# First attention of a transformer kernel: queries and keys split into high and low parts, scores in three passes

## What is computed

```python
h = rms_norm(x, norm_mix[l])
aq, ak, av, bq, bk, bv, cq = jnp.split(h @ w_in[l], offsets, axis=-1)
aq = rms_norm(aq.reshape(b, t, A_HEADS, 2, A_HEAD_DIM), a_q_norm[l])      # 4 heads, 2 components, 64
ak = rms_norm(ak.reshape(b, t, A_HEADS, 2, A_HEAD_DIM), a_k_norm[l])
...
def one_block(args):                                # 128 queries
    s = jnp.einsum('bqhcd,bkhcd->bhcqk', qb, k).astype(jnp.float32) * scale
    s = s - slopes[None, :, None, None, None] * dist[None, None, None]
    p = jax.nn.softmax(s, axis=-1)
    p_diff = p[:, :, 0] - lam * p[:, :, 1]
    return jnp.einsum('bhqk,bkhe->bqhe', p_diff.astype(v.dtype), v)
```

## Time and profile before

| | us |
|---|---|
| median of the 3 runs | 3133.65 |
| lowest and highest | 3133.06, 3135.37 |
| the profiled execution, its device time | 3138.5 |
| its span in the profile | 3136.7 |
| PE busy, of the span | 3070.3 |
| third attention with head 0's query and key tiles | from about 139 to 215 |
| first attention, first to last scores | 204 to 494 |

### The profile page before, as it was taken

One profiled execution on the slowest core, in us unless ns is written; L12 is line 12 of the kernel. 1 busy time (PEld: TensorE's weight loads), 2 busy tenths in 40 slices (PEclk: granted clock), 3 DMA queues, 4 the chain that ended last, 5 costly groups with the idle time before them and its releaser, 6 DMA issues.

```text
span 3136.7 us, 50320 instructions
## 1 busy us (share of the span) xinstructions
PE 3070.3 (98%) x18600; PEld 2611.5 (83%) x18600; DVE 1795.4 (57%) x3577; ACT 1333.8 (43%) x2641; POOL 648.6 (21%) x870
## 2 busy tenths in 40 slices
PE   7999999999999999999999999998999999999999
PEld 7988888999999888888788887887977777687777
DVE  6557674353344332345788886876353666753675
ACT  5446565454445221232333333455433555522452
POOL 3424334453541000001111111000101011032240
PEclk9999999999999999999999999999999999999999
DMA  5110011011111221122232225643100000221012
GB/s 204 37 48 18 21 36 51 28 62 51 59 49 54 95 77 51 51 106 79 73 111 106 101 101 200 201 150 132 53 28 22 16 28 15 108 68 70 28 61 101
DMA packets 77412, 231.27 MB, mean 74 GB/s; under 512 B 17712, under 2 KB 21936, under 8 KB 65648
## 3 DMA queue, kind: packets, MB, share of 16 engines
q1 hardware_dynamic: 77168, 228.05, 20.9%
HBM read 183.92 MB, written 43.84 MB: 73 GB/s over the span
## 4 chain that ended last, share of the span: by engine, by line
PE 89%; DVE 6%; ACT 2%; issue 1%; DMA 1%; SPq 0%; POOL 0%; DVEq 0%; ACTq 0%; POOLq 0%
PE ps L2545 70%; PE ps L2588 7%; PE ps L2596 3%; PE ps L2552 2%; PE ps L2603 2%; PE ps L2619 2%; PE ps L2611 1%; PE ps L2622 1%; PE ps L2639 1%; DVE wlo L2814 0%; DVE hlo L2891 0%; ACT hhi L2659 0%; DMA wd<-in_WD 0%; ACT whi L2649 0%; DVE qk L2922 0%
## 5 line engine op out<-in xcount | busy, mean ns | idle before, releaser
L2545 PE MATMUL ps<-whi,hhi 128*128 128x256 f32 (+2 forms) x1920 | 581.1, 303 | 1.4 <-DVE hlo L3016 1.0
L2545 PE MATMUL ps<-whi,hlo 128*128 128x256 f32 (+2 forms) x1920 | 564.4, 294 | 0.0
L2545 PE MATMUL ps<-wlo,hhi 128*128 128x256 f32 (+2 forms) x1920 | 564.2, 294 | 0.0
L2545 PEld LDWEIGHTS ps<-whi,hhi 128*128 128x128 f32 x1920 | 368.7, 192 | 11.2 <-issue 3.4
L2545 PEld LDWEIGHTS ps<-wlo,hhi 128*128 128x128 f32 x1920 | 369.1, 192 | 7.6 <-issue 0.2
L2545 PEld LDWEIGHTS ps<-whi,hlo 128*128 128x128 f32 x1920 | 368.6, 192 | 7.8
L3153 POOL TENSOR_SCALAR stats<-stats 128x2 f32<-128x2 f32 (+2 forms) x230 | 59.5, 259 | 1434.8 <-ACT xsf L2653 511.9
L2545 PE MATMUL ps<-hhi,whi 128*128 128x512 f32 x864 | 342.3, 396 | 0.0
L2545 PE MATMUL ps<-hhi,wlo 128*128 128x512 f32 x864 | 337.0, 390 | 0.0
L2545 PE MATMUL ps<-hlo,whi 128*128 128x512 f32 x864 | 336.3, 389 | 0.0
L3142 POOL CAST whi<-raw 128x512 fp32r<-128x512 f32 (+4 forms) x172 | 109.0, 634 | 649.8 <-PE ps L2545 640.4
(11 more groups left out here) (616 smaller groups left out, 7013.3 us busy)
## 6 DMA issues: line engine op xcount, KB each, us to landing
raw<-in_W SPq DMA_DIRECT2D x61, 1024.0 KB, 4.9
scratch_fs<-fo SPq DMA_DIRECT2D x77, 256.0 KB, 2.0
raw<-in_W SPq DMA_DIRECT2D x24, 768.0 KB, 4.2
wd<-in_WD SPq DMA_DIRECT2D x44, 256.0 KB, 3.3
wf0b<-in_WF SPq DMA_DIRECT2D x10, 1024.0 KB, 5.2
wf1b<-in_WF SPq DMA_DIRECT2D x10, 1024.0 KB, 5.2
scratch_x<-x SPq DMA_DIRECT2D x16, 512.0 KB, 3.4
orw<-scratch_outs SPq DMA_DIRECT2D x6, 1024.0 KB, 5.6
```

Source lines behind the costliest of these rows:

```text
L2545: x = e.matmul(r.out, a, b, start=(r.start and m == 0), stop=(r.stop and m == n - 1), skip_group_check=r.joined)
```

## The change

Queries and keys of the first attention are kept as a high and a low part of type fp32r, and a score group takes three passes (high keys by high queries, low by high, high by low) in the place of float32 products. Two blocks of 256 keys that lie side by side become one of 512: in 48 of the 64 groups; in 16 they stay two blocks. ACT writes the high part of each as before, and DVE makes the low part from PSUM and the high part, two new instructions of 128 columns for each of the 32 tiles; the second of these now sets free the turn's bank and tells that the tile is ready. The queries move from two whole heads to a ring of twelve tiles; the exponentials of the second component get buffers of their own (`aF`, two of 1024), `aE` is three of 1024, `aPT` two instead of three.

```diff
         def qk_out(q):
             q.frees = [flat(free() if callable(free) else free) for _, _, free in q.outs]
+            q.two = isinstance(q.outs[0][0], tuple)
+            q.hi_done = [signal("qk_hi") for _ in q.outs] if q.two else []
             emit("qk_out", q)
             q.done(q.turned.read)
...
                     u.ei, u.E, u.E_free = self.E.take()
+                    u.halves = [u.E]
+                    if self.E2.bufs:
+                        u.e2i, u.E2, free = self.E2.take()
+                        u.halves.append(u.E2)
+                        u.E_free = u.E_free + free
...
-        aq = [rest(f"aq{i}", [T], F, 8 * KB * i) for i in range(2)]
-        ak = [rest(f"ak{i}", [T], F, 8 * KB * i + 4 * KB) for i in range(2)]
+        aq = [[rest(f"aq{n}{i}", [128], R, o + 512 * n) for n in range(2)] for i, o in enumerate(aq_at)]
+        ak = [[rest(f"ak{i}{n}", [T], R, o[n] * KB) for n in range(2)] for i, o in enumerate(((0, 4), (36, 60)))]
...
-        aE = [rest(f"aE{i}", [2 * T], F, (40 + 8 * i) * KB) for i in range(3)]
-        aPT = [rest(f"aPT{i}", [T], F, (28 + 4 * i) * KB) for i in range(3)]
+        aE = [rest(f"aE{i}", [T], F, (40 + 4 * i) * KB) for i in range(3)]
+        aE2 = [rest(f"aF{i}", [T], F, (52 + 4 * i) * KB) for i in range(2)]
+        aPT = [rest(f"aPT{i}", [T], F, (28 + 4 * i) * KB) for i in range(2)]
...
-                qk_evac(t, p, 64, [(aq[h % 2][:, cut], aq_gain[:, h:h + 1], lambda: a_scored(h - 2)),
-                                   (ak[h % 2][:, cut], col("a_k_norm"), None)],
+                n = 8 * h + t
+                q_free = lambda: a_units[n - 12].s_full if n >= 12 else c_free
+                qk_evac(t, p, 64, [(tuple(x[:, :] for x in aq[n % 12]), aq_gain[:, h:h + 1], q_free),
+                                   (tuple(x[:, cut] for x in ak[h % 2]), col("a_k_norm"), lambda: a_scored(h - 2))],
...
-                        pieces.append(([q[half, cut]] * 2, [k[half, 256 * x:256 * x + 256] for x in res[p:p + 2]], bias))
+                        x, y = res[p:p + 2]
+                        keys = [sl(256 * x, 512)] if y == x + 1 else [sl(256 * x, 256), sl(256 * y, 256)]
+                        pieces.append(([tuple(w[half, :] for w in q)] * len(keys), [tuple(w[half, c_] for w in k) for c_ in keys], bias))
... (PE)
+                            for j, (a_, b_) in enumerate(((0, 0), (0, 1), (1, 0))):
+                                for p in r.parts:
+                                    q, k = p.blocks[b]
+                                    x = e.matmul(p.place.ps[:, o:o + n], q[a_], k[b_], start=j == 0, stop=j == 2)
... (ACT)
+                        if r.two:
+                            e.activation(dst[0], v, ACT.Copy, scale=gain).then_inc(w.sig(r.hi_done[x]), 1)
+                            continue
... (DVE)
+                elif kind == "qk_out" and r.two:
+                    for x, (dst, gain, _) in enumerate(r.outs):
+                        w.wait_ge(*w.last)
+                        w.wait_each(r.hi_done)
+                        v = r.turned.ps[:, x * 128:(x + 1) * 128]
+                        a = e.scalar_tensor_tensor(dst[1], v, gain, dst[0].bitcast(F), ALU.mult, ALU.subtract)
+                        a.then_inc(w.sig(r.turned.read) if x else w.inner(), 1)
```

More of the change, by code:

```diff
@@ L645, in build, with __init__ @@
         class Att:
-            def __init__(self, E, PT, os_, sb, ob, dve_turns=True, together=False, paired=False, by_feature=False, between=False):
+            def __init__(self, E, PT, os_, sb, ob, dve_turns=True, together=False, paired=False, by_feature=False, between=False, second=()):
                 self.by_feature, self.between = by_feature, between
@@ L657, in __init__ @@
                 self.dve_turns, self.together, self.paired = dve_turns, together, paired
-                self.turn = 0
+                self.turn, self.E2 = 0, Slots(second)
             def scores(self, *us):
@@ L683, in scored @@
                         r.blocks = list(zip(q, rhs)) if isinstance(q, list) else [(q, rhs)]
-                        r.n = sum(k.shape[-1] for _, k in r.blocks)
-                        r.out, r.mx = u.E[:, at_[x]:at_[x] + r.n], mxs[x][:, p:p + 1]
+                        r.n = sum(width(k) for _, k in r.blocks)
+                        r.out, r.mx = u.halves[comp.half][:, at_[x]:at_[x] + r.n], mxs[x][:, p:p + 1]
                         at_[x] += r.n
@@ L695, in scored @@
                     x_ = Rec()
-                    x_.u, x_.e, x_.scored, x_.mx = u, u.E[:, comp.col:at_[x]], r.place.read, mx
+                    x_.u, x_.e, x_.scored, x_.mx = u, u.halves[comp.half][:, comp.col:at_[x]], r.place.read, mx
                     if u.kept:
@@ L731, in combine @@
                 u.e_ready = [u.mixed]
+                self.E2.free[u.e2i] = [u.mixed]
             def probs(self, u):
@@ L823, in unit, with comp, width @@
             return u
-        def comp(col_, pieces):
+        def comp(col_, pieces, half=0):
             c = Rec()
-            c.col, c.pieces = col_, pieces
+            c.col, c.pieces, c.half = col_, pieces, half
             return c
+        def width(k):
+            return (k[0] if isinstance(k, tuple) else k).shape[-1]
         def post_plain(self, u):
@@ L1080, in build @@
             for qt in range(8):
-                q, k, tb = aq[h % 2], ak[h % 2], atab
+                q, k, tb = aq[(8 * h + qt) % 12], ak[h % 2], atab
                 res, at_ = key_order(qt)
-                cut = slice(qt * 128, (qt + 1) * 128)
                 comps = []
@@ L2585, in _ @@
                     for b in range(len(r.parts[0].blocks)):
-                        n = r.parts[0].blocks[b][1].shape[-1]
+                        n = width(r.parts[0].blocks[b][1])
+                        if isinstance(r.parts[0].blocks[b][0], tuple):
+                            for j, (a_, b_) in enumerate(((0, 0), (0, 1), (1, 0))):
+                                for p in r.parts:
+                                    q, k = p.blocks[b]
+                                    x = e.matmul(p.place.ps[:, o:o + n], q[a_], k[b_], start=j == 0, stop=j == 2)
+                                    if j == 2 and b == len(p.blocks) - 1:
+                                        x.then_inc(p.place.full[0], 1)
+                            o += n
+                            continue
                         for p in r.parts:
@@ L2934, in _ @@
                             if len(p.bias.shape) == 3:
-                                src, out = [a.rearrange("p (g c) -> p g c", g=len(p.blocks)) for a in (src, out)]
+                                src, out = [a.rearrange("p (g c) -> p g c", g=p.bias.shape[1]) for a in (src, out)]
                             x = e.tensor_tensor_reduce(out=out, in0=src, in1=p.bias, scale=-u.scale, scalar=3e38,
```

15 lines of the change are left out of this document (9 added, 6 removed).

## The result

| us | before | after |
|---|---|---|
| median, with the number of runs | 3135.26 (10) | 3143.72 (10) |
| lowest and highest | 3133.06, 3138.05 | 3141.77, 3146.54 |
| profiled execution: device time, span | 3138.5, 3136.7 | 3141.77, 3140.0 |
| first scores of the first attention | 204.46 | 211.92 |
| its last unit's second score group | 492.79 | 501.87 |

The changed kernel is slower: ratio of the times 1.0029, 95% interval 1.0021 to 1.0036, which is 8.5 us. The profiles put it where it was looked for: up to the first scores 7.46 us are lost, from there to the last unit's second group 1.62, together 9.08.

The account below looks back on a forecast made before the run. PE's queue was taken as the bound. Third attention +6.7, first attention's one-tile units +5.7, savings -5.6 and -0.3, head starts +1.0 gave +7.5 us on the median 3133.65: 3141 us; 8-in-10 range 3128 to 3153.

Parts of the forecast that it names:

- the bank's release at the turn of `cE`: Third attention, head 0: the bank has no slack, so PE stands still 0.84 us longer at 8 tiles, +6.7 us.
- the ring of ACT and DVE: First attention, units with one query-key tile: waits between ACT and DVE set 9.11 us against PE's 8.33; together +5.7 us.
- the step on two-tile units: First attention, six units with two query-key tiles: PE doesn't wait for DVE and each keeps the 0.35 us saving.
- Score groups: First attention: fp32r halves overlap, groups take 0.89 us, or 0.92 split, saving 0.35 us a unit.
- The low parts, each, and the third attention: DVE takes 0.351 us per low part; the bank is free 0.84 us after ACT's last high part, +6.7 us over 8 tiles.
- The ninth: First attention, one-tile unit behind the second head's start: starts with 0.8 us of slack, so costs 0.
- the waits spread: Rival, first attention: DVE's delay also reaches two-tile units and high parts wait longer; +5 on the sum, 3146 us, chance 0.07.
- Starts of heads: Second and fourth heads: scores wait for the last key tile; low parts add 0.84, the unit saves 0.35; +1.0 us together.
- halves halfway between together and in turn: Rival, score groups: an fp32r pair takes 0.34 us, about +17 for the groups, 3153 us; chance 0.07.
- only the third attention pays: Rival: first attention's ACT-DVE waits are looser, PE keeps all 11 us there; -4.5 us, 3129 us, chance 0.20.
- no wait shows: Rival: waits in the first and third attention stay hidden and only the passes count; 3122 us, chance 0.06.
- halves in turn: Rival, score groups: array halves alternate in fp32r, groups take 1.58 and 1.64 us; 3176 us, chance 0.10.

Follow-up runs that it names:

- low parts from a copy: Changed kernel, but ACT writes float32 copies to SBUF and frees the bank; high and low parts are made from the copy: 3139.56 us, ratio 1.0016 to before.
- the form with both moves: Copy-based kernel with the last two tiles of heads 1 to 3 made directly from PSUM, and ACT's copied high parts behind the square: 3131.99 us, ratio 0.9989 to before.
- The form with the one move alone: Copy-based kernel with the last two tiles of heads 1 to 3 made directly from PSUM, ACT's high parts still ahead of the square: 3134.06 us, ratio 0.9995 to before.

## Why the prediction was right

It said 3141, +7.5 us, slower; the time is +8.5 in the medians, +9.1 at the end of the stage in the traces. The measured 3143.72 lies 2.7 above the 3141, and 1.6 of these are the median of before, which rose from 3133.65 to 3135.26 with more runs. The two mechanisms on which it rests, the bank's release at the turn of `cE` and the ring of ACT and DVE, are what the runs show. That the sum came so near is in part luck: the step on two-tile units was wrong by 2.2 us, and the ring came out 1.3 us better than said. By its own steps:

- *Score groups.* 0.89 and 0.92 us were said, 0.89 and 0.91 measured. The row that was nearest, the same group in float32, told it; the share of the page didn't. The saving of 0.35 us a unit comes nearly in full where nothing waits: 0.31 to 0.34 in ten of the 12 units with other tiles, 0.17 and 0.18 in the two shortest. The sum had 11.2 for all units; without low parts the profiles show 9.1 in this stage, and the 12 us between the medians are more than that.
- *The low parts, each, and the third attention.* 0.351 us each, all 64 of them alike. 0.84 us for a tile became 0.87, and 6.7 became 6.87 (low parts in head 0 alone) to 7.46. Doubling them moved the first scores by 6.33, for 6.2. This term rested on one thing, that the bank had no slack, and the eight small waits of the earlier trace rows were its sign.
- *The ring.* 9.11 us were added up from single rows of before, and DVE's ring is 9.11 to 9.13 long. PE's periods were 8.96 to 9.08: a little less, because the units around have slack that is used up first. Four of the five middle ones paid 2.7 us together; the fifth I had taken for a query-key tile holds a value tile beside a turn, and saved 0.3 instead. The first three paid 3.7, of which 1.7 are a fall of the clock: 2.0 for 1.8. The ninth paid 0.06 for 0.
- *Two tiles: the step that failed.* "In 11.41 us the ring has time, DVE ends 0.8 us later but PE doesn't wait." PE does wait. Four of the five units of the table (I had counted six) saved 0 to 0.2 us instead of 0.35, and one lost 0.4; together they lost 0.1 where 2.1 had been counted as saved. I had followed the ring and not the bank. With two tiles both banks for turns are taken, and the turn of `aO`, third in the row, needs the first one's bank, which DVE now leaves 0.4 us behind the second turn's start. The turn of `aO` waits seven times for low parts, 2.5 us in all. It is the mechanism of the third attention at a second place; a rival ("the waits spread") put the delay of these units at +5, it was +2.2.
- *Starts of heads.* +0.58 each, 1.16 for 1.0.
- *Not in the sum:* the third head's start fell from 14.73 to 13.06. It isn't the change; that execution of before had a fall of the clock there.
- *A slip in a rival:* for halves halfway between together and in turn the prediction has "about +17" for the groups. Its own terms give +11, midway between -11.2 and +33.6, and it is with +11 that its 3153 us comes out.

The sum over the first attention: +1.62 measured, +0.8 said. The two-tile units made it 2.2 us worse than said, the ring (less its fall of the clock) 1.3 better, the rest is small; the fall in after and the one in before cancel.

Of the rivals, "only the third attention pays" falls with the periods of 9 us, "no wait shows" with the turn of `cE`, and both forms of halves in turn with the groups of 0.89.

What stays open: the form that beats both kernels is still 1.5 us slower at the second head's start than the run without low parts. Its longer wait before the scores explains 0.6 of these and the wait at the turn of `aO` 0.7. In the profiles its first attention is 7.6 us longer than without low parts: 3.4 are falls of the clock, 3.0 the two heads' starts, 1.1 the units just ahead of them. Whether the falls come with the waits, no run tells. Giving each low part its own high part to wait for, and not both, would shorten the chain by some 0.4 us, an estimate from the 0.40 us between the starts of ACT's two high parts; it wasn't tried, because DVE and ACT would then read one bank of PSUM at the same time without an order between them.

## What to carry to other kernels

Before you put work between a PSUM bank's last reader and its release, list who takes that bank next in PE's order, in every kind of unit: at the turn of `cE` the price was the whole added time, because a small wait of 0.3 us already stood there, and at the turn of `aO` it was the part that the slack didn't cover. Copy out first, release, then refine from the copy (here 3132 us against 3144); and give that refining a place in each queue behind whatever another engine waits for. The ring through two engines could be added up here from rows of the old profile to 0.02 us, and it shows whether a saving on a third engine can appear at all.

## What the runs showed of the hardware

**The clock fell after PE had stood still, and a fall in this stage cost 1.7 us.** PE's granted clock in stretches of 2 us (the value behind POOL's group: 1.00 is 2.4 GHz, 0.50 is 1.2), first after, around the group at 239.34 us that had waited 2.72 us, then before, around its turn at 333.21 that had waited 1.84:

```profile
238.00:240.00 2.00, 0.66 (x10) 0.69 (x12) 1.82 (x5) 0.00 (x0) 0.00 (x0) 0.95 0.56 135
240.00:242.00 2.00, 2.00 (x13) 1.78 (x12) 1.77 (x7) 0.25 (x1) 0.63 (x2) 0.50 0.91 381
242.00:244.00 2.00, 2.00 (x14) 2.00 (x13) 1.90 (x5) 1.47 (x3) 1.32 (x3) 0.69 0.05 16
```

```profile
332.00:334.00 2.00, 0.79 (x7) 0.82 (x8) 1.00 (x3) 0.62 (x3) 1.92 (x2) 0.97 0.00 0
334.00:336.00 2.00, 2.00 (x11) 2.00 (x11) 0.00 (x0) 0.95 (x4) 0.20 (x1) 0.50 0.49 78
336.00:338.00 2.00, 2.00 (x13) 1.86 (x11) 0.00 (x0) 0.00 (x0) 0.00 (x0) 0.67 0.92 389
```

What a stretch loses is its length times one less the clock: 1.7 us for each of these, and the period of 14.73 us against 13.06 shows the same 1.7. Some falls last twice as long and lose 3.4. The waits that preceded a fall in the first attention were of 1.4 to 3.7 us, but not each such wait had one (2.0 us at the same turn without low parts: none). In the first attention the runs without low parts for heads 1 to 3 had no fall in three profiles; before lost 1.7 us to the clock there, the changed kernel 1.7, the other forms with low parts there 1.7 to 6.8.

At another place a fall cost nothing that shows. Before the first scores the execution of before lost 3.4 us to the clock and those of four forms with no low parts from PSUM in head 0 lost 1.7, and yet the first scores came at 204.46 in the one and at 203.68 to 204.73 in the others (no low parts, low parts in heads 1 to 3, low parts from a copy, and the form with both moves). The form with the one move alone lost 3.4 too, with the first scores at 204.64.

Over the whole span the loss was 15.6 us in the profiled execution of before and 8.0 in that of after. Behind the first attention it was 10.5 and 4.5 us; less that, the 2643.9 and 2638.1 us are 2633.5 and 2633.6. This agreement is closer than the method: over all eleven profiles, whose code is the same there, the part behind spreads over 6.0 us, and over 4.1 with the loss taken off. So the clock explains a part of such differences, and it should be summed up before two spans are compared.

**DVE with both operands in SBUF slows down beside POOL.** 128 columns took 0.29 us alone and 1.23 beside POOL's split of weights (rows of the first form from a copy, above). Of its 64 low parts 52 took 0.29 us, and the 12 others, 0.63 to 1.33 us, all ran beside that split. The mix of 1024 columns took 2.42 there, where its shortest in the stage of before is 1.28. The low parts read from PSUM, in the changed kernel, took 349 to 353 ns, all 64 of them, though 15 ran beside the split of weights:

```profile
L2947 DVE SCALAR_TENSOR_TENSOR ak<-ps,cols,ak 128x128 fp32r<-128x128 f32 x32 | 11.2, 351 | 1.1
L2947 DVE SCALAR_TENSOR_TENSOR aq<-ps,stats,aq 128x128 fp32r<-128x128 f32 x32 | 11.2, 351 | 32.8 <-ACT ak L2703 32.4
```

The Trainium skill (SBUF — State Buffer, SBUF: two separate sides) says that a DVE instruction with two inputs in SBUF and a GpSimd one that reads SBUF exclude each other for the whole instruction; the 1.23 us, ending 0.15 us behind POOL's row, agree. So work moved from PSUM to a copy in SBUF is faster alone, and exposed to POOL.
